# U blocks of a two-layer PEER kernel: one 512-column matmul for both input parts, their halves added by VectorE, the panels' remainders taken by GpSimd

## The reference

```python
def block(xb):
    q = (xb @ w_q).reshape(PEER_BLOCK, PEER_HEADS, PEER_QDIM)
    s1 = jnp.einsum('phd,nd->phn', q[..., :half], subkeys[0])
    s2 = jnp.einsum('phd,nd->phn', q[..., half:], subkeys[1])
    ...
    cs, ci = lax.top_k(cand, PEER_TOPK)
    ...
    g = jax.nn.softmax(cs.astype(jnp.float32), axis=-1)
    u = u_tab[e]
    a = jax.nn.gelu(jnp.einsum('pd,phkd->phk', xb, u).astype(jnp.float32), approximate=False)
    return jnp.einsum('phk,phkd->pd', g * a, v_tab[e].astype(jnp.float32)).astype(xb.dtype)
```

## Time and profile before

| | us |
|---|---|
| runs, median of 3 (lowest, highest) | 2613.04 (2612.5, 2615.88) |
| the profiled execution | 2613.86 |
| its span | 2612.0 |
| TensorE matmuls busy | 2536.4 (97%) |
| VectorE busy | 1767.5 (68%) |
| ScalarE busy | 1239.3 (47%) |
| GpSimd busy | 79.4 (3%) |
| U stage, layer 0 and layer 1 | 789.3 to 1219.9 and 1806.5 to 2237.1 |

### The profile page before, as it was taken

How to read it: one execution, slowest core, us unless ns; L and a number is a source line. 1 busy time by engine, 2 the same in 40 slices (tenths; PEclk the granted TensorE clock), 3 DMA queues, 4 the chain that set the end, 5 groups by cost and what they waited for, 6 DMA issues and landing times.

```text
span 2612.0 us, 43051 instructions
## 1 busy us (share of the span) xinstructions
PE 2536.4 (97%) x15972; PEld 2268.9 (87%) x15972; DVE 1767.5 (68%) x3535; ACT 1239.3 (47%) x2429; POOL 79.4 (3%) x42
## 2 busy tenths in 40 slices
PE   8999999999999999999999998999999999999997
PEld 4587889988889999999888887679999999888886
DVE  3672668865359977786788874538986777555554
ACT  2322124342244467775444443333547776555554
POOL 0000000000050000000000000014000000000000
PEclk9999999999999999999999999689999999999998
DMA  6562567656334544344777754122554344555553
GB/s 262 193 242 81 203 228 279 235 203 238 116 129 148 183 173 142 135 145 163 272 280 275 270 218 150 49 97 99 188 182 158 134 145 143 183 192 192 193 193 111
DMA packets 65351, 471.69 MB, mean 181 GB/s; under 512 B 7296, under 2 KB 7552, under 8 KB 8240
## 3 DMA queue, kind: packets, MB, share of 16 engines
q1 hardware_dynamic: 64656, 467.85, 49.6%
q10 hardware_dynamic: 272, 1.05, 0.1%
q0 software_dynamic: 272, 0.69, 0.1%
HBM read 468.51 MB, written 1.05 MB: 180 GB/s over the span
## 4 chain that ended last, share of the span: by engine, by line
PE 93%; DVE 5%; ACT 1%; issue 1%; DMA 0%; SPq 0%; DVEq 0%
PE bank L648 27%; PE bank L723 27%; PE bank L510 6%; PE bank L880 5%; PE bank L660 4%; PE bank L789 4%; PE bank L675 3%; PE bank L911 2%; PE bank L520 2%; PE bank L1017 2%; PE bank L494 1%; PE bank L456 1%; PE bank L974 1%; DVE macc L1625 1%; PE bank L526 1%
## 5 line engine op out<-in xcount | busy, mean ns | idle before, releaser
L648 PE MATMUL bank<-h_split,t_split 128*128 128x256 f32 x6144 | 771.8, 285 | 4.8 <-DVE t_split L1857 4.8
L648 PEld LDWEIGHTS bank<-h_split,t_split 128*128 128x128 f32 x6144 | 745.5, 191 | 6.8 <-DVE t_split L1857 6.1
L1857 DVE TENSOR_TENSOR t_split<-ring,t_split 128x1024 fp32r<-128x1024 f32 x512 | 624.6, 1221 | 159.0 <-ACT t_split L1185 157.5
L723 PE MATMUL bank<-t_split,w_split 128*128 128x512 f32 x3072 | 703.9, 390 | 0.0
L723 PEld LDWEIGHTS bank<-t_split,w_split 128*128 128x128 f32 x3072 | 574.7, 188 | 118.9
L1190 ACT ACTIVATE t_split<-ring 128x1024 fp32r<-128x1024 f32 x256 | 271.6, 1061 | 357.9 <-PE bank L723 290.2
L1185 ACT ACTIVATE t_split<-ring 128x1024 fp32r<-128x1024 f32 x256 | 271.1, 1059 | 294.1 <-PE bank L648 273.9
L1889 DVE TENSOR_TENSOR w_split<-arena,w_split 128x256 fp32r<-128x256 f32 x256 | 108.8, 425 | 223.6 <-ACT w_split L1192 223.6
L1112 ACT ACTIVATE arena<-bank 128x256 f32<-128x256 f32 (+2 forms) x160 | 64.3, 405 | 352.1 <-PE bank L675 67.5
L1625 DVE SCALAR_TENSOR_TENSOR macc<-ring,cact,macc 128x256 f32<-128x256 f32 x336 | 162.9, 485 | 12.0
L880 PE MATMUL bank<-h_split,wd_split 128*128 128x256 f32 x1056 | 129.4, 284 | 4.0 <-ACT h_split L1412 4.0
(11 more groups left out here) (298 smaller groups left out, 2815.8 us busy)
## 6 DMA issues: line engine op xcount, KB each, us to landing
ring<-in_peer_u SPq DMA_DIRECT2D x128, 1024.0 KB, 4.9
ring<-in_peer_v SPq DMA_DIRECT2D x128, 1024.0 KB, 4.9
ring<-in_w_mod SPq DMA_DIRECT2D x24, 1024.0 KB, 5.0
ring<-in_mod_w SPq DMA_DIRECT2D x24, 1024.0 KB, 4.9
arena<-in_mod_w SPq DMA_DIRECT2D x24, 1024.0 KB, 6.5
ring<-in_w_in SPq DMA_DIRECT2D x22, 1024.0 KB, 4.9
ring<-in_w_up SPq DMA_DIRECT2D x22, 1024.0 KB, 5.0
ring<-in_peer_wq SPq DMA_DIRECT2D x16, 1024.0 KB, 5.0
```

The source lines that it names most:

```text
L648: last = mm(bank[:, 0:T], u[:, a_, k, :], h_split[:, b_, k, :], start=(k == 0 and a_ + b_ == 0), stop=(k == KT - 1 and a_ == 1))
L723: last = mm(BK[2 * tt + hf][:, :], w_split[:, j, a_, tt * P:(tt + 1) * P], t_split[:, 1 - j, b_, hf * 512:(hf + 1) * 512], start=(first an ...
L1857: TT(t_split[:, 1 - j, 1, :].rearrange("p (k c) -> p k c", k=KT), ring[:, r, :].rearrange(view, k=KT, j=2)[:, j], t_split[:, 1 - j, 0, :]. ...
```

## The change

In the U stage three things are different.

- TensorE multiplies the panel's rounded part with both parts of the tokens in one matmul of 512 columns, eight of them; the halves go to columns 0 to 255 and 256 to 511 of the bank. The eight matmuls of the panel's remainder stay as they were, on the first half.
- The two halves are added: ScalarE copies the second half into a new SBUF tile `half_t`, ahead of its next rounding, and VectorE adds it to the first half in the bank (`add`). The GELU waits for the add.
- The remainder is subtracted by GpSimd (`lo_u`) instead of VectorE, with a semaphore of its own, `split_u`, which TensorE and SyncE's loads of this stage wait for. GpSimd's DMAs of `subT`, `pos` and `band` now stand behind the 128 subtractions of layer 0. The V stage's subtractions stay with VectorE.

```diff
--- hidden (TensorE)
-                    for a_, b_ in ((0, 0), (0, 1), (1, 0)):
-                        if a_ == 1:
-                            pe.wait_ge(sems["split"], e.more("split"))
-                        for k in range(KT):
-                            last = mm(bank[:, 0:T], u[:, a_, k, :], h_split[:, b_, k, :],
-                                      start=(k == 0 and a_ + b_ == 0), stop=(k == KT - 1 and a_ == 1))
+                    both = bank[:, :].rearrange("p (s t) -> p s t", s=2)
+                    for k in range(KT):
+                        mm(both, u[:, 0, k, :], h_split[:, :, k, :], start=(k == 0), stop=False, skip_group_check=True)
+                    pe.wait_ge(sems["split_u"], e.more("split_u"))
+                    for k in range(KT):
+                        last = mm(bank[:, 0:T], u[:, 1, k, :], h_split[:, 0, k, :], start=False, stop=(k == KT - 1), skip_group_check=True)
--- SyncE, loads of u
-                        sync.wait_ge(sems["split"], i * 4 + (split + 2 * r + 2))
+                        sync.wait_ge(sems["split_u"], i * 4 + (split + 2 * r + 2))
--- gelu (ScalarE)
+                    act.wait_ge(sems["added"], BLOCKS * l + b + 1)
--- ScalarE, the loop over blocks
                     if b >= 2:
                         act.wait_ge(sems["proj"], done + b - 1)
+                        if b < BLOCKS + 2:
+                            A(half_t[:, b % 2, :], BK[4 + e.tile % 2][:, T:2 * T], ACT.Copy).then_inc(sems["halved"], 1)
--- VectorE
+                def add(b):
+
+                    bank = BK[4 + (tile_before + b) % 2]
+                    dve.wait_ge(sems["halved"], BLOCKS * l + b + 1)
+                    TT(bank[:, 0:T], bank[:, 0:T], half_t[:, b % 2, :], ADD).then_inc(sems["added"], 1)
...
                 for tt in range(2):
-                    lo(0, tt, "p (k j c) -> p j k c")
                     pick(PH - 2, tt)
                 e.tiles("proj", 16)
-                for b in range(BLOCKS + 3):
-                    if 2 <= b < BLOCKS:
-                        lo(b // 2 % 2, b % 2, "p (k j c) -> p j k c")
+                tile_before = e.tile
+                for b in range(2, BLOCKS + 3):
+                    if b < BLOCKS + 2:
+                        add(b - 2)
--- GpSimd
+            def lo_u(l):
+
+                def block(r, j, count):
+
+                    pool.wait_ge(sems["hi"], count)
+                    pool.tensor_tensor(t_split[:, 1 - j, 1, :].rearrange("p (k c) -> p k c", k=KT),
+                                       ring[:, r, :].rearrange("p (k j c) -> p j k c", k=KT, j=2)[:, j],
+                                       t_split[:, 1 - j, 0, :].rearrange("p (k c) -> p k c", k=KT).bitcast(f32), SUB
+                                       ).then_inc(sems["split_u"], 1)
+
+                with pool.Fori(0, PAIRS // 2) as i:
+                    for b in range(4):
+                        block(b // 2, b % 2, i * 4 + (2 * BLOCKS * l + b + 1))
+
             for h in range(PH):
                 lo_q(0, h)
+            lo_u(0)
             pool.wait_ge(sems["ranked"], 2 * PH)
             pool.dma_start(subT, a["subT"][1]).then_inc(sems["sub_in"], 16)
```

More of the change, by code:

```diff
@@ L147, in build @@
         macc = sb("macc", [P, 3, T])
+        half_t = sb("half_t", [P, 2, T])
         arena_at = nc.sbuf_base
@@ L179, in build @@
                   "mod_acc", "mod_turn", "mod_bank", "proj", "turn", "bank4", "bank5", "sq", "ms", "var", "std", "h",
-                  "q_hi", "q_lo", "hi", "split", "lb", "gate", "gates_f", "logf", "expo", "exps", "lin_in",
+                  "q_hi", "q_lo", "hi", "split", "split_u", "lb", "gate", "gates_f", "logf", "expo", "exps", "lin_in",
                   "scores", "masked", "dstate", "state", "o_sum", "o_bank0", "o_bank1", "osq", "oms", "ovar", "ostd",
@@ L184, in build @@
                   "peer_sm", "peer_ex", "routes", "ranked", "rank_bank0", "rank_bank1", "rank_bank2", "rank_bank3",
-                  "p2", "p2_act", "square", "g_mm", "g_gate", "g_store", "negated", "mixed", "w_hi", "w_ready", "w_free0", "vpad",
+                  "halved", "added", "p2", "p2_act", "square", "g_mm", "g_gate", "g_store", "negated", "mixed", "w_hi", "w_ready", "w_free0", "vpad",
                   "mod_row", "mod_cols", "att_sfree", "hs", "vvar", "vstd", "modulated", "wexp", "cums", "zln", "up_hi", "up_lo", "h_lo", "hf_hi", "hf_lo", "wd_hi", "wd_lo", "down", "x_new", "xstd", "mod_in0", "mod_in1"]
@@ L375, in _ @@
                     sync.dma_start(ring[:, r, :], u[r]).then_inc(sems[f"loaded{r}"], 16)
-                split = 2 * BLOCKS * layer
+                split = BLOCKS * layer
                 with sync.Fori(0, PAIRS // 2 - 1) as i:
                     for r in range(2):
-                        sync.wait_ge(sems["split"], i * 4 + (split + 2 * r + 2))
+                        sync.wait_ge(sems["split_u"], i * 4 + (split + 2 * r + 2))
                         sync.dma_start(ring[:, r, :], u[i * 2 + (r + 2)]).then_inc(sems[f"loaded{r}"], 16)
                 for r in range(2):
-                    sync.wait_ge(sems["split"], split + BLOCKS - 2 + 2 * r)
+                    sync.wait_ge(sems["split_u"], split + BLOCKS - 2 + 2 * r)
                     sync.dma_start(ring[:, r, :], v[r]).then_inc(sems[f"loaded{r}"], 16)
@@ L386, in v_pairs @@
                     for r in range(2):
-                        sync.wait_ge(sems["split"], at * 4 + (split + BLOCKS + 2 * r + 2))
+                        sync.wait_ge(sems["split"], at * 4 + (split + 2 * r + 2))
                         sync.dma_start(ring[:, r, :], v[at * 2 + (r + 2)]).then_inc(sems[f"loaded{r}"], 16)
@@ L1884, in mix @@
                     TT(part, part, gelu_t[:, b % 2, 0:n], MUL).then_inc(sems["mixed"], 1)
+                e.skip("hi", BLOCKS)
                 def value_lo(b, at):
@@ L2412, in _ @@
                 lo_q(1, h)
+            lo_u(1)
 def kernel(**inputs):
```

## The result

The changed kernel takes **2676.99 us** (median of 4 runs, 2674.06 to 2681.12) against 2612.88 (4 runs, 2612.5 to 2615.88): a ratio of 1.0242, 95% interval 1.023 to 1.0254. Its profiled execution has a span of 2674.4 us against 2612.0.

A forecast was written before the change was run, and what follows sets the result against it. The prediction took TensorE to bound the U and V stages, with VectorE near full only in the ranking. Its terms, +50 + 16 − 4 − 5 + 3 = +60 us on 2613.9, gave 2674 us, range 2584 to 2710.

The forecast's parts named there:

- the harmless-looking rows of GpSimd: Profile rows: two GpSimd subtractions took 4.67 us with VectorE nearly idle, 4.76 beside its picks.
- rival 1: U stage: GpSimd and VectorE don't disturb each other, TensorE stays the bound; 2588 us, chance 0.29.
- The gate stretch, +50: Gate blocks: mutual exclusion of GpSimd and VectorE adds 0.39 us to each of 128 blocks, +50 us.
- 2.38 + 1.68 + 0.1 = 4.15 us per block: Gate blocks: subtraction, then VectorE's mixing, gates and one-hots, then hand-over, in turn; 4.15 us against 3.76.
- rival 2: Gate stretch: the engines exclude each other, but VectorE fits in GpSimd's gap, blocks at 3.66 us; 2610 us, chance 0.13.
- My own test for failure: Layer 0, 957 to 994 us: TensorE still busy for all of it would mean the forecast failed.
- Ranking +16: Ranking stretch, 45 blocks a layer: exclusion and delayed adds cost +8 us a layer, +16 us.
- picks −5: Ranking's picks: TensorE no longer waits for VectorE's late subtraction, −5 us.
- slot turns +3: Gateless U blocks: refilling a panel slot takes 11.0 to 11.3 us against 11.1 for four blocks, +3 us.
- The matmuls, −27: U blocks: eight 512-column matmuls replace sixteen of 256, saving 0.107 us a block over 256 blocks, −27 us.
- Rival 3: Gateless blocks: GpSimd's subtraction is slower on eight separate runs than on one; 2636 us at 3.2 us each, chance 0.10.

The follow-up runs named there:

- run 3: Changed kernel with the eight long two-tensor ranking steps per layer replaced by one-tensor reductions of the same size: 2652.67 us.
- run 4: Changed kernel with the gate stretch's one-hots and mixing replaced by one-tensor reductions of the same sizes: 2631.01 us.
- run 7: Changed kernel with the long ranking steps, one-hots and mixing all replaced by one-tensor reductions: 2610.72 us.
- run 2: Kernel before the change with only the U remainders' subtraction moved to GpSimd; 24 matmuls of 256 columns, no copy, no add: 2625.61 us.
- run 6: Changed kernel without the copy and the add, so one product is left out; GpSimd subtracts: 2613.6 us.
- run 9: Complete changed kernel with only VectorE's order altered, the one-hots ahead of the mixing: 2629.99 us.
- The square: Table of stage (blocks 0 to 55) and gate pace for the changed kernel, run 6, run 7 and run 8: with or without add, two-tensor steps kept or replaced.
- run 8: Changed kernel with ranking steps, one-hots and mixing replaced by one-tensor reductions, and without copy and add: 2591.5 us.
- Run 5: Kernel before the change with the eight 512-column matmuls, VectorE subtracting, no copy or add, one product left out: 2594.99 us.
- run 11: As run 10, but GpSimd subtracts the remainders of blocks 0 to 5 of each layer: 2595.5 us.
- run 10: Mixed version: VectorE subtracts; blocks 0 to 48 as in the kernel before, the 512-column form with copy and add from block 49: 2598.65 us.

## Why the prediction was right

2674 us were forecast, 2677 measured, and that the two engines exclude each other is what the forecast took against the harmless-looking rows of GpSimd. But that the total is so near is luck: the gate stretch was forecast 12 us too high and blocks 0 to 55 some 14 us too low, and the chain by which the gate stretch loses was another.

- **Exclusion against none (rival 1).** Right, and shown twice: by the stretched rows next to the unstretched reduction, and by runs 3, 4 and 7, which put reductions in place of the stretched instructions and gain 24, 46 and 66 us.
- **The gate stretch, +50.** Measured +37.7. The step of the prediction that failed is the turn "2.38 + 1.68 + 0.1 = 4.15 us per block". It took it that every subtraction waits for VectorE's mixing, gates and one-hots, and loses in every block. Time is lost in one block of three; the others run at 3.69 and 3.80, the mean is 4.06. The chain named with it (one-hots, add, GELU, bank) was wrong too: among the gates TensorE waits for the one-hots themselves, 36.5 us in all, and for the bank 0.2. The add does matter, since runs 2 and 6, which have the exclusion but no add, lose nothing here. As far as the rows show, it matters through what stands behind it: the mixing comes later, meets the next subtraction, and delays the gates and the one-hots. The forecast did not ask for another order of VectorE's queue, and it is the order that decides: run 9 has every operation of the kernel, fits them in GpSimd's gap as in rival 2, and gets to 3.705, within 0.01 us of TensorE's own pace.
- **My own test for failure** was badly chosen. From 957 to 994 TensorE is busy for 36.84 of 37 us, almost what I had said would refute me: the gates begin at 968 here, and their first blocks run undisturbed while the mixing is short. 1010 to 1050 shows the loss.
- **Blocks 0 to 55.** Ranking +16, picks −5, slot turns +3 × 56/64 and the matmuls of 22 blocks −2.4 came to +11; measured +25.6. The term that was too small is the add's: the forecast charged it only where a ranking step is stretched, 8 us a layer. The square shows 8 to 9 us for copy and add with the long steps unstretched too (TensorE's waits for the bank are 15.7 us in run 7 and 2.6 in run 8), and 9 to 10 for the long steps on top. Two waits of some 2.1 us in the 8 to 9 stand behind VectorE's first ranking step and behind a stretched TENSOR_SCALAR with a long step after it, as shown at the square; the rest was not taken apart.
- **The matmuls, −27.** Eight of 512 columns take 1.84 us in the U blocks, from 1227.34 to 1229.18 below, 0.230 each and not 0.2267; a block's pitch is 2.79, where 2.77 was forecast. Run 5 gains 19 us, not 27, 0.074 per gate block instead of 0.107. The Trainium skill's 2.5 ns (TensorE: Matmul & The Clock Gate, "Wait — 56ns, not 53.3ns?") gave an estimated 5 us; the runs don't bear it out.

```profile
1227.34 2.00 PE L647 MATMUL bank<-h_split,t_split 128*128 128x512 f32 x8
1229.18 1.11 PE L650 MATMUL bank<-h_split,t_split 128*128 128x256 f32 x8
1230.13 2.00 PE L647 MATMUL bank<-h_split,t_split 128*128 128x512 f32 x8
```

- **The picks, −5.** Right in kind: GpSimd in blocks 0 to 5 alone (run 11 against 10) takes 3.2 and 2.6 us off the two layers' stages.
- **Rival 3 and the slot turns, +3.** The panel's eight separate pieces cost GpSimd nothing: its median is 2.406 us, and 2.407 for the query panels in the same trace. In run 8, where GpSimd still subtracts but neither add nor long two-tensor steps are left, the stage is 159.8 / 162.1 against 56 × 2.79 = 156: 4 and 6 us a layer for the slots' turns and all else. How much of it is the slots' was not separated.

## What to carry to other kernels

Before work is given to an idle GpSimd, list the VectorE instructions beside it that read two SBUF tensors, and the one-tensor kinds named below. Ask of each who waits for it and for what stands behind it in VectorE's queue; the stretch costs nothing if no one waits there, and a new order of the queue may be all it needs. A saving on the bounding engine that puts an in-order step (here the add) on a full engine's queue is paid for there, so use it only in the stretches where that engine has room: 2595.5 us came from that. Test a forecast in the middle of a stretch, not at its start.

## What was not expected

- VectorE instructions that read one SBUF tensor are stretched too, if they are of certain kinds: a CAST of 128 columns (0.22 us) lasted 2.44 beside a subtraction and the 128-column TENSOR_SCALAR (0.34) up to 2.57, while a 2.28 us reduction was never touched. In run 9 such a pair ends 0.35 us after the subtraction, one short instruction's length.
- Exclusion and add, each harmless alone among the gates (0.02 and 0.01 us a block), cost 0.37 us a block together, while in blocks 0 to 55 their costs simply add up.
